# Grouping the tokens of a routed mixture on the chip, so that each expert runs on its group's tiles

## What is computed

```
p_group = softmax(t @ w_rg + b_rg);  g_val, g_idx = top_1(p_group)          # one of 4 groups for each token
e_val, e_idx = top_2(expert logits of that group)                            # 2 of its 4 experts
gate[t, e] = g_val * softmax(e_val) at the two experts, 0 elsewhere          # 16 experts
for e in range(16):
    hidden = silu(t @ w_gate[e]) * (t @ w_up[e])                             # 1024 -> 256
    y = y + gate[:, e:e+1] * (hidden @ w_down[e])                            # 256 -> 1024
```

## Time and profile before

| what | value |
|---|---|
| median of 3 runs | 1653.41 us (1653.02 to 1654.69) |
| span of the profiled execution | 1650.3 us |
| instructions | 24634 |
| busy PE / DVE / ACT / POOL | 96% / 54% / 43% / 8% |
| loaded from HBM | 239.55 MB, 146 GB/s over the span |

### The profile page before, as it was taken

The page is one execution under the profiler, slowest core; times in us unless marked ns, Lnnn a source line. Parts: engine busy times, 40 slices in busy tenths (PEclk is TensorE's granted clock), DMA queues, the critical chain, the costliest instruction groups (busy, mean ns, idle before and its releaser), DMA issues.

```text
span 1650.3 us, 24634 instructions
## 1 busy us (share of the span) xinstructions
PE 1592.3 (96%) x10537; PEld 1359.5 (82%) x10537; DVE 885.5 (54%) x1198; ACT 707.1 (43%) x1034; POOL 128.8 (8%) x146
## 2 busy tenths in 40 slices
PE   7999999999999999998899999999999998899998
PEld 6976997998888888854677888888878975799998
DVE  4633664756544466977735333333337667565554
ACT  5536533444544435456723222221225447443433
POOL 3001000000000014610200000000001320000000
PEclk9999999999999999999999999999998999999999
DMA  9577557466565634373342333332244350355551
GB/s 292 154 252 233 167 174 248 154 195 196 159 207 182 192 86 160 101 231 103 26 129 87 97 99 102 102 95 85 89 141 128 103 175 30 110 174 182 187 179 65
DMA packets 228917, 242.19 MB, mean 147 GB/s; under 512 B 13064, under 2 KB 222440, under 8 KB 228808
## 3 DMA queue, kind: packets, MB, share of 16 engines
q1 hardware_dynamic: 226672, 238.03, 45.0%
q0 software_dynamic: 1600, 2.37, 2.3%
q10 hardware_dynamic: 536, 0.22, 0.1%
HBM read 239.55 MB, written 1.05 MB: 146 GB/s over the span
## 4 chain that ended last, share of the span: by engine, by line
PE 86%; DVE 6%; ACT 4%; issue 1%; DMA 1%; SPq 1%; DVEq 0%; ACTq 0%
PE bank L680 18%; PE bank L682 18%; PE bank L681 18%; PE bank L1830 4%; PE bank L1837 4%; PE bank L1836 3%; PE score_banks L1167 2%; PE score_banks L1903 2%; PE score_banks L1904 2%; PE score_banks L1905 2%; PE bank L1201 2%; DVE small L1242 1%; DVE w_lo L669 1%; PE bank L788 1%; PE bank L753 1%
## 5 line engine op out<-in xcount | busy, mean ns | idle before, releaser
L669 DVE TENSOR_TENSOR w_lo<-raw,w_hi 128x2048 fp32r<-128x2048 f32 (+1 forms) x147 | 337.0, 2295 | 232.9 <-ACT w_hi L657 232.5
L680 PE MATMUL bank<-xn_hi,w_hi 128*128 128x256 f32 (+1 forms) x1232 | 406.9, 330 | 5.3 <-ACT proj L1653 3.1
L681 PE MATMUL bank<-xn_lo,w_hi 128*128 128x256 f32 (+1 forms) x1232 | 404.1, 328 | 0.0
L682 PE MATMUL bank<-xn_hi,w_lo 128*128 128x256 f32 (+1 forms) x1232 | 404.0, 328 | 0.0
L657 ACT ACTIVATE w_hi<-raw 128x2048 fp32r<-128x2048 f32 (+1 forms) x147 | 277.1, 1886 | 155.7 <-PE bank L682 97.8
L680 PEld LDWEIGHTS bank<-xn_hi,w_hi 128*128 128x128 f32 x1232 | 235.4, 191 | 27.1 <-issue 4.6
L682 PEld LDWEIGHTS bank<-xn_hi,w_lo 128*128 128x128 f32 x1232 | 235.4, 191 | 20.2
L681 PEld LDWEIGHTS bank<-xn_lo,w_hi 128*128 128x128 f32 x1232 | 235.5, 191 | 19.9
L680 PE MATMUL bank<-hid_hi,w_hi 128*128 128x256 f32 (+1 forms) x416 | 137.5, 331 | 2.6 <-DVE hid_lo L1735 1.9
L681 PE MATMUL bank<-hid_lo,w_hi 128*128 128x256 f32 (+1 forms) x416 | 136.4, 328 | 0.0
L682 PE MATMUL bank<-hid_hi,w_lo 128*128 128x256 f32 (+1 forms) x416 | 136.4, 328 | 0.0
(11 more groups left out here) (336 smaller groups left out, 2673.5 us busy)
## 6 DMA issues: line engine op xcount, KB each, us to landing
raw<-in_w_ada SPq DMA_DIRECT2D x48, 1024.0 KB, 5.8
raw<-in_w_in SPq DMA_DIRECT2D x30, 1024.0 KB, 6.1
raw<-in_w_gate SPq DMA_DIRECT2D x22, 1024.0 KB, 5.3
raw<-in_w_up SPq DMA_DIRECT2D x22, 1024.0 KB, 5.4
raw<-in_w_exp_up SPq DMA_DIRECT2D x16, 1024.0 KB, 7.3
raw<-in_w_exp_gate SPq DMA_DIRECT2D x16, 1024.0 KB, 9.5
raw<-in_w_exp_down SPq DMA_DIRECT2D x16, 1024.0 KB, 5.1
raw<-in_w_down SPq DMA_DIRECT2D x16, 1024.0 KB, 5.3
```

The lines of the kernel that those rows point to most:

```text
L669: dve.tensor_tensor(w_lo[:, r % RAW_SLOTS, 0:k * cols], raw[:, r % RAW_SLOTS, 0:k * cols], w_hi[:, i % HIGH_SLOTS, 0:k * cols].bitcast(F32 ...
L680: pe.matmul(o, s_hi, m_hi, start=i == 0, stop=False)
L681: pe.matmul(o, s_hi, m_lo, start=False, stop=False)
L682: last = pe.matmul(o, s_lo, m_hi, start=False, stop=i == n - 1)
```

## The change

The tokens are sorted into slots by their group, on the chip. PE sums a one-hot of the groups (totals, and a triangular product for each token's place in its group). DVE ranks the four groups by size, writes their order as four integers, and places the tokens: the largest group from slot 0, the second behind it but not before slot 128, the third from slot 256 and the fourth behind that. So there are 3 tiles of 128 slots, and `RANK_TILES` says which of them a rank can touch: rank 0 tiles 0 and 1, rank 1 tile 1, ranks 2 and 3 tile 2.

The normed tokens (hi and lo) are turned to rows by 32 transposes, 8 behind each xo tile (the last 8 after the router's sums), and a one-hot matrix (`pick_slots`, 256 x 384) gathers them by 32 matmuls of 384 columns; ACT and DVE copy the results to where the experts read. The experts run by rank: SP reads the order into registers (`load_order`), and each expert's load has a source address with the register in it (`expert_weights`). Each expert runs only on the tiles of its rank: 48 or 24 matmuls in the pair, 4 or 2 transposes, and in `pe_down` the hidden values are the weights and 512 columns of `down` move: 24 or 12 matmuls. The gates are gathered to slots too (`pe_slot_gates`). The sums of a slot tile are split when its last expert is done (after experts 3, 7 and 15), and scattered back by the turned one-hot (`pe_scatter`): two tiles in expert 10, 32 matmuls of 256 columns, the third after expert 15, 16 matmuls.

Moved: the router's matmuls go between the xo tiles; eight conditioning tiles go from the second block's attention (steps 4 to 7 and 17 to 20) to between the last xo tile and expert 0, 5 of them before the matmuls that count the groups and 3 after; the norm of the context goes from experts 2 to 6 to experts 1 to 3. Expert 0's weights are now issued after the order is known, in halves.

The core of the diff:

```diff
...
+SLOT_TILES = 3
+SLOTS = SLOT_TILES * P
+RANK_TILES = ((0, 1), (1,), (2,), (2,))
...
+ADA_ORDER = [(0, j) for j in range(22)] + [(1, j) for j in range(8)] + [(0, 22), (0, 23)] \
+    + [(1, j) for j in range(8, ADA_TILES)]
...
+_plan_ada("gap", 7, range(8))
 _plan_ada(("norm", "n1", 0), 4, [0, 0])
-_plan_ada(("mix", 0), 1, range(8), range(17, 21))
+_plan_ada(("mix", 0), 1, range(4))
...
+        def expert_weights(name):
+
+            rank, j = divmod(name[1], PER_GROUP)
+            w = a["w_exp_" + name[0]][0].rearrange("(g j) (k p) c -> j p g k c", j=PER_GROUP, p=P)[j]
+            return w[:, bass.ds(chosen[rank], 1), :, :].rearrange("p g k c -> p (g k) c")
+
+        def load_order(sp):
+
+            sp.wait_ge(*order_ready.at("order"))
+            for rank in range(GROUPS):
+                chosen.append(sp.value_load(order[0:1, rank:rank + 1], min_val=0, max_val=GROUPS - 1))
...
+                if name == ("up", 0):
+                    sp.wait_ge(*tile_used.at(tiles[r + 1 - RAW_SLOTS][0]))
+                    load_first_pair(sp, r)
+                elif name == ("gate", 0):
+                    pass
+                elif name[0] in ("gate", "up", "down"):
+                    sp.dma_start(dst, expert_weights(name)).then_inc(*raw_loaded[r % RAW_SLOTS].mark(name, 16))
...
+                for i, tile in enumerate(tiles_of(e)):
+                    o = expert_bank(e, i)[:, :]
+                    x_hi, x_lo = slot_input(tile, c)
                     halves_of = o.rearrange("p (m f) -> p m f", m=2)
-                    pe.matmul(halves_of, x_hi[:, c, ts], hi, start=c == 0, stop=False, skip_group_check=True)
+                    pe.matmul(halves_of, x_hi, hi, start=c == 0, stop=False, skip_group_check=True)
                     if lo is None:
                         for m, slot in enumerate(raw_slots(names)):
-                            pe.matmul(halves_of[:, m, :], x_hi[:, c, ts], w_lo[:, slot, cols], start=False, stop=False,
+                            pe.matmul(halves_of[:, m, :], x_hi, w_lo[:, slot, cols], start=False, stop=False,
                                       skip_group_check=True)
                     else:
-                        pe.matmul(halves_of, x_hi[:, c, ts], lo, start=False, stop=False, skip_group_check=True)
-                    last = pe.matmul(halves_of, x_lo[:, c, ts], hi, start=False, stop=c == KC - 1, skip_group_check=True)
+                        pe.matmul(halves_of, x_hi, lo, start=False, stop=False, skip_group_check=True)
+                    last = pe.matmul(halves_of, x_lo, hi, start=False, stop=c == KC - 1, skip_group_check=True)
...
+                if h == 1:
+                    between()
+                cs = slice(h * 512, (h + 1) * 512)
+                for i, tile in enumerate(tiles_of(e)):
+                    o = y_bank(tile, h)[:, :]
+                    for k in range(2):
+                        first, stop = e == first_of[tile] and k == 0, e == last_of[tile] and k == 1
+                        pe.matmul(o, h_hi[:, k, i, :], hi[:, k, cs], start=first, stop=False, skip_group_check=True)
+                        pe.matmul(o, h_hi[:, k, i, :], lo[:, k, cs], start=False, stop=False, skip_group_check=True)
+                        last = pe.matmul(o, h_lo[:, k, i, :], hi[:, k, cs], start=False, stop=stop, skip_group_check=True)
...
+        def pe_scatter(pe, c, slot_tiles):
+
+            o = scatter_bank(c // 2)[:, (c % 2) * S:(c % 2 + 1) * S]
+            for tile in slot_tiles:
+                at = lambda v: y_rows(v, tile, c // 4)[:, c % 4 // 2, (c % 2) * P:(c % 2 + 1) * P]
+                pe.matmul(o, at(hid_hi), pick_tokens[:, tile, :], start=tile == 0 and c % 2 == 0, stop=False, skip_group_check=True)
+                last = pe.matmul(o, at(hid_lo), pick_tokens[:, tile, :], start=False, stop=tile == 2, skip_group_check=True)
+            return last
...
+        def pe_rows_turned(pe, j):
+
+            pe.wait_ge(*(xn_ready.at(("ffn",)) if j == 3 else normed.at((("ffn",), j))))
+            if j >= 2:
+                pe.wait_ge(*rows_high.at(j - 2))
+                pe.wait_ge(*rows_low.at(j - 2))
+            for o, src in zip(turn_banks(j), expert_in):
+                for t in range(ST):
+                    for i in range(2):
+                        last = pe.transpose(o[:, t * S + i * P:t * S + (i + 1) * P],
+                                            src[:, 2 * j + i, t * P:(t + 1) * P].bitcast(F32), ident)
+            last.then_inc(*rows_turned.mark(j))
...
+        gather_bank = lambda n: bank[n % 6][:, 0:SLOTS]
+
+        def pe_gather(pe):
+
+            pe.wait_ge(*rows_high.at(3))
+            pe.wait_ge(*rows_low.at(3))
+            pe.wait_ge(*dve_misc.at("pick slots"))
+            for c in range(KC):
+                for i, v in enumerate((hid_hi, hid_lo)):
+                    n = 2 * c + i
+                    if c >= 3:
+                        pe.wait_ge(*(gathered_low if i else gathered_high).at(c - 3))
+                    for t in range(ST):
+                        rows = v[:, t * 4 + c // 2, (c % 2) * P:(c % 2 + 1) * P]
+                        last = pe.matmul(gather_bank(n), rows, pick_slots[:, t, :], start=t == 0, stop=t == 1)
+                    last.then_inc(*gathered.mark((c, i)))
...
+        def act_gathered(act):
+
+            for c in range(KC):
+                src = gather_bank(2 * c)
+                act.wait_ge(*gathered.at((c, 0)))
+                act.activation(xn_hi[:, c, 0:S], src[:, 0:S], ACT.Copy)
+                act.activation(hid_hi[:, c, S:S + P], src[:, S:SLOTS], ACT.Copy).then_inc(*gathered_high.mark(c))
...
+        def pe_counts(pe):
+
+            pe.wait_ge(*dve_misc.at("group one"))
+            tri, ones = const("negtri"), const("negtri")[:, 0:1].broadcast_to([P, P])
+            pe.matmul(TOTALS, ones, group_ones[:, 0, :], start=True, stop=False, skip_group_check=True)
+            pe.matmul(TOTALS, ones, group_ones[:, 1, :], start=False, stop=True, skip_group_check=True)
+            pe.matmul(COUNTS, tri, group_ones.rearrange("p t g -> p (t g)"), start=False, stop=False, skip_group_check=True)
+            pe.matmul(COUNTS[:, 0:GROUPS], ones, group_ones[:, 1, :], start=False, stop=True, skip_group_check=True)\
+              .then_inc(*counted.mark("groups"))
...
+            own.ready(dve.scalar_tensor_tensor(out=count_keys, in0=TOTALS, scalar=float(GROUPS), in1=rank_const,
+                                               op0=ALU.mult, op1=ALU.subtract))
+            own.ready(dve.tensor_tensor(square(below), along(count_keys), down(count_keys), ALU.is_ge))
+            own.ready(dve.tensor_reduce(ranks, square(below), AX.X, ALU.add))
+            own.ready(dve.tensor_tensor(square(in_rank), along(ranks), down(rank_const), ALU.is_equal))
+            own.ready(dve.tensor_tensor(square(rank_parts), square(in_rank), along(rank_const), ALU.mult))
+            own.ready(dve.tensor_reduce(rank_group, square(rank_parts), AX.X, ALU.add))
+            dve.tensor_scalar(order, rank_group, -1.0, float(GROUPS), ALU.mult, ALU.add).then_inc(*order_ready.mark("order"))
...
+            load_order(sp)
+            load_tiles(sp, tile_at["up", 0], len(tiles))
...
+                if j > 0:
+                    pe_rows_turned(pe, j - 1)
+                    pe_router_chunks(pe, 2 * j - 2)
+            pe_ada(pe, ada_planned("gap", 0))
+            pe_router_chunks(pe, KC - 2)
+            pe_ada(pe, ada_planned("gap", 1))
+            pe_token_moment(pe)
+            pe_rows_turned(pe, 3)
+            for step in range(2, 5):
+                pe_ada(pe, ada_planned("gap", step), step)
+            pe_counts(pe)
+            for step in range(5, 8):
+                pe_ada(pe, ada_planned("gap", step), step)
+            pe_gather(pe)
...
+            act_columns_guess(act, ("ffn",), token_moment, token_rstd)
+            act_rows_high(act, 3)
+            act_gathered(act)
...
+            dve_columns_rstd(dve, ("ffn",), token_moment, token_rstd, token_new)
+            dve_router_groups(dve)
+            dve_rows_low(dve, 3)
+            dve_slots(dve)
+            dve_gathered(dve)
...
```

More of the change, by code:

```diff
@@ L164, in weight_tiles @@
         add(("xo", j), a["w_xo"][0], 0, D, j * TILE_C)
+    for step in range(8):
+        ada(planned("gap", step))
     for e in range(EXPERTS + 1):
         if e < EXPERTS:
-            pair = [(("gate", e), a["w_exp_gate"][0, e]), (("up", e), a["w_exp_up"][0, e])]
-            for name, w in reversed(pair) if e == 0 else pair:
-                add(name, w, 0, D, 0)
+            for kind in ("up", "gate") if e == 0 else ("gate", "up"):
+                tiles.append(((kind, e), None, KC, TILE_C))
         if e > 0:
-            add(("down", e - 1), a["w_exp_down"][0, e - 1], 0, D_EXP, 0, D)
+            tiles.append((("down", e - 1), None, D_EXP // P, D))
     for l in range(LAYERS):
@@ new lines, in pe_down, with y_done, act_y_high @@
+            last.then_inc(*tile_used.mark(name))
```

(11 more changed lines are left out.)

374 lines of the change are left out of this document (272 added, 102 removed).

## The result

The changed kernel takes 1627.5 us (median of 4 executions, 1618.9 to 1632.0), the kernel before beside it 1654.1 (1653.0 to 1655.3): a ratio of 0.983, 95% interval 0.981 to 0.985. That is 26.6 us less, where 47 were forecast. 1627.5 lies at the upper end of the range and is nearest to rival (b), 1626. The profiled execution took 1625.6 us with a span of 1623.8. The executions of the changed kernel lie 13 us apart. The four of the kernel before lie 2 apart, but in a longer series thirteen of them lay 8 apart (1652.0 to 1660.3), so this isn't a trait of the change.

A forecast was written before the change was run, and what follows sets the result against it. PE, busy 96%, was taken as the bound. From 304.1 us the terms gave 240.9 us against 281.8, 40.9 less; with 6 less in the attention, 47 together: 1653.4 - 47 = 1606 us, range 1586 to 1628.

The forecast's parts named there:

- (b): Rival: loads or clock are worse, 12.7 us for ten light experts and 5 us more of gap; 1626 us, chance 0.27.
- One expert, and what is late next: Light experts: PE needs 8.5 us each, but weights are late next, so 10.7 us each, 11.2 with the clock.
- L: Light experts: landing of the up tile, 11.3 us after the end of pair e-1, 8.8 of it flow of weights.
- item 6: Second block's attention without eight conditioning tiles: 6 us less, bounds 2 and 10; small POOL loads already inside the 8.8 us.
- The half microsecond for each expert: Light experts: half of the 1.0 us that a half-clock stretch costs each, raising 10.7 to 11.2 us.
- Item 1: Between the xo tiles: turned normed rows and router chunks on PE add 3.3 us.
- Item 2: Gap from last xo tile to expert 0, waiting for grouping, gather and splits: 27.3 us, 2.5 of it for the clock.
- Items 3 and 4: Expert 0 to end of pair 3: 58.4 us; pair 3 to pair 15: 134.1, plus 4.5 for splits and scatter.
- Item 5: Tail from pair 15's end to the moments: 13.3 us, 8.1 of it before the last down product.
- (c): Rival: runtime addresses make loads slow, so sorting saves matmuls but not time; slower than before, chance 0.04.
- (a): Rival: light experts run near the PE bound, 10.2 us each, and the gap is 22 us; 1590 us, chance 0.17.
- three signs: Prediction wrong if order comes over 12 us after last xo, a lone load lands after over 6, or clock stays half.

The follow-up runs named there:

- half_load: Changed kernel loading only the first half of each gate and up tile from expert 5 on, with the same work on PE, ACT and DVE: 1603.1 us.
- best_c: Changed kernel with no conditioning tiles in the gap, no early split of the next projection's tile, and small POOL loads behind xq and xo tiles: 1620.5 us.
- pool_early: Changed kernel with the sixteen small POOL loads issued during experts 0 to 3, four behind each, instead of one behind every expert: 1627.2 us.
- light_fill: Changed kernel with eight unused matmuls of 512 columns added on PE ahead of each pair from expert 5 to 15: 1627.6 us.
- ada0: Changed kernel with all eight moved conditioning tiles put back into the second block's attention: 1620.9 us.
- tail: Changed kernel where ACT and DVE split the next projection's first tile after the last expert's hidden rows instead of ahead of them: 1627.0 us.
- static: Changed kernel with the experts' order written into the program, so no register loads and fixed weight addresses: 1624.0 us.
- ada5: Changed kernel with five conditioning tiles left in the gap and three put back into the attention: 1624.9 us.

## Why the prediction was right and wrong

**One expert, and what is late next.** Right. A light period isn't PE's 8.5 us; weights bound it, as half_load shows. The landing L of the up tile, forecast at 11.3 us behind the end of pair e-1, is 11.3 to 12.5 us for experts 5 to 15 in best_c, 11.7 in the mean (470.7 to 482.0 is the shortest). With the small loads, in the changed kernel, it is 11.6 to 13.4, 12.5 in the mean (507.2 to 520.3, for one). In half_load it is 8.6 to 10.0. The step that failed is the last sentence of item 6: that the small POOL loads are inside the 8.8 us of flow. They are 2% of the bytes, but each can stop the flow for 2 us. The light stage came out near its forecast in the profiled execution (140.4 for 138.6), and at 141.3 to 149.1 in the six other profiles with all bytes and the small loads among them, so that nearness is in part luck. The periods aren't the even 11 us that were forecast either, but 8.4 to 16.3 us, one short behind one long, 11.7 on average. Without the pieces ten experts took 113.5 to 114.3 us in four profiles; with them 117.3 to 124.8 in seven. That is the clean separation that the argument rests on. The Trainium skill, "DMA: Bandwidth & Descriptors", "Why small descriptors are slow (HBM only)", gives 27% of overhead to pieces of 256 bytes. By it and the 350 GB/s of the flow a load of 64 KB would take 0.26 us, an estimate. The 7 us that four of them added to one tile in pool_early are far from that, so this overhead isn't what stops the flow; what does, no run shows.

**The clock.** The half microsecond for each expert was a fair term: four stretches in twelve light experts, 1.7 us each, is 0.6. light_fill didn't turn it into a gain. The Trainium skill, "TensorE: Matmul & The Clock Gate", "HAM oscillation — how this bites in real kernels", tells of a loop that loses the clock anew at each tile. This case isn't that loop: in the changed kernel the clock was lost behind the four longest holes (2.8 to 4.3 us) and kept behind those of 1.4 us and less. Nor is a hole's length all that decides: in best_c one of 2.0 us was followed by a half-clock stretch and one of 2.6 by none.

**Item 1.** 3.3 us for the turned rows and router chunks: right (26.5 us from the first to the last xo matmul, before 23.0: 3.5). That it starts from 280.8 was wrong by 2.9.

**Item 2, the gap.** Group, counts, order and picks came at t + 8.6, 10.3, 11.8 and 14.1, for 7.8, 9.0, 10.6 and 13.5. The term that failed is the conditioning tiles 5 to 7, "in by 13 to 14.5". It took a load's landing alone, 5.1 us. Four were issued within 7.5 us, so the last three land 3.0 us apart, the last one 7.96 us after its issue, and its own 1.9 us on PE at half clock comes behind: the gather starts at t + 17.6 in place of 13.7 (20.0 less the gather's 5.6 and the copies' 0.7). ada0 measures it: 4.2 us. The register loads were 3.1 us for the 1.5 taken; hidden, as forecast.

**Items 3 and 4.** The 2.5 us for the clock stood in the gap, but fell on expert 0, which did start at half clock. Counted in item 3, pairs 0 to 3 took 60.5 for 58.4 + 2.5: right. The light experts are above.

**Item 5, the tail.** Forecast 13.3 with "DVE being busy with two whole splits. That stays". Both splits did stay, but the second belongs to the next projection, whose load is issued when a slot comes free; a period that shrank from 17 to 8 us left the load no time. It landed at 545.8, and ACT and DVE, in order, kept the last hidden rows waiting: 10.2 us from pair 15 to its down product in place of 8.1, and 2.5 us of half clock on top. The edit tail shows it: 11.2 in all.

**Item 6, the attention.** Taken at 6 less, with bounds of 2 and 10. The term that was mis-sized: up to the end of the attention the move saves 3.3 us on average over the profiles, 0.4 for each tile where the forecast had 0.75 and the sign to look for was 1, and 1.8 in the changed kernel's profile against that of before. So 4.2 of the 6.9 us missed in this stage lie here. Most of the other 2.7 is the late loss in the second block, for which the forecast had no term and no run a cause. The chain of the earlier trace rows named PE at each unit; that a piece of PE on the chain isn't saved whole because DVE and ACT stand close behind is a guess that no run tests. The stage is the largest part of the miss.

**The rivals.** (b) was right in its number, and in its first half (the gap 4 us longer). The other half, 15 us by 12.7 us a light expert, wasn't there: it came to 11.7 in the profiled execution. In its place stand the tail (4.9), the rest (6.9) and the later start (2.9), which no rival named. The measured time lies half a microsecond inside the range, whose upper end was drawn for other reasons, so that it holds is partly luck. (c) fell: static. (a) fell: no profile came near 10.2 us a light expert while 3.15 MB were loaded. Of the three signs that would have made the prediction wrong none came: the order was known 11.8 us after the last xo tile for the limit of 12, a load alone landed in 5.1 us, and the clock came back.

## What to carry to other kernels

When a stage goes from PE-bound to load-bound, look for every other transfer in it, however few its bytes: here loads of 64 KB in 256-byte pieces, one at a time and unseen as long as PE paced the stage, cost some 1 to 2 us each and moved from place to place with their price until they met an idle queue. Cost a load by what is queued ahead of it, not by its landing alone, and look at each in-order engine for work that waits for a load ahead of work that doesn't. Where work fills a hole, ask whether its own loads are in time.

## What the runs showed of the hardware beyond what was expected

- A 64 KB load from POOL's queue in 256-byte pieces makes a hole of 2 us in the flow of 1 MB loads of SP's queue, some 5 us behind its issue; four of them took a tile from 8.3 to 15.4 us.
- Four register loads on SP and what surrounds them took 3.1 us, and a load with a runtime address 0.37 us of issue and the same time to land as a fixed one.
- The light stage took 140.4 to 147.7 us in four kernels that leave it as it is (changed, ada0, ada5, tail), one profile each, so a difference of a few us there needs a separation such as that of the column ten.
